# Dilated attention layer: v as two token panels kept on chip, 56 feature tiles in 14 panels, the gates placed behind the keys, three projection banks

## The chip, the cores and the metric

One Trainium2 chip, of which the program uses one core. The time is the device time of one execution in microseconds, the median of several executions. Engines are named as the profile names them: PE (TensorE), PEld (its weight loads), ACT (ScalarE), DVE (VectorE), POOL (GpSimd), SP (SyncE, which here only starts transfers). PSUM, where PE writes, has eight banks of 128 partitions by 512 float32.

## The reference, cut to what matters

Four layers run one after the other on 512 tokens of width 1024: a mixer, a mixture of experts, a short convolution, and the dilated attention layer that the change is about. That last one computes, with h the normalised and modulated input:

```python
def dilated_mixer(h, w_in, w_out, cos, sin):
    B, S, _ = h.shape                       # 1, 512
    G, H, Dh = len(DIL_RATES), DIL_HEADS, DIL_HEAD_DIM      # 3, 8, 128
    E = H * Dh
    q, k, v, z = jnp.split(h @ w_in, [G * E, 2 * G * E, 2 * G * E + E], axis=-1)
    q = apply_rope(q.reshape(B, S, G, H, Dh), cos, sin)
    k = apply_rope(k.reshape(B, S, G, H, Dh), cos, sin)
    v = v.reshape(B, S, H, Dh)
    ...   # per rate g: banded attention of q[g], k[g], v; the three mixed by softmax of their log-denominators
    y = o.reshape(B, S, E).astype(h.dtype) * jax.nn.silu(z)
    return y @ w_out
```

So each head needs eight products of 1024 x 128 weights with the input: three queries, three keys, one v and one gate z. A gated residual and a last normalisation follow.

## The kernel before

Weights come in panels of 2 MB (128 partitions x 4096 float32), number 114 (`P_DIL`) to 129 for this layer's input projection, 130 and 131 (`P_DO`) for its output projection. SP's queue loads them in order into the four slots of `ring`; `load` (L1956) waits until the last chunk of the panel that lay in the slot before has been read. A panel has four chunks. ACT copies each chunk to a rounded high part (`hi`, L746) and DVE computes the rest (`lo`, L1171), into two buffers that alternate, so chunk c can be split only when PE is done with chunk c-2.

PE knows two ways to use a panel. `feature_tiles` (L288) gives the result by feature: a chunk is 128 output columns, and a tile is 24 matmuls (8 of the high part, 8 of the low part, 8 of the high part against the input's low part) of 512 moving columns into one bank. `token_panel` (L306) gives it by token: four tiles of 128 tokens by 512 output columns that fill four banks together, a chunk being 256 rows of the weights; 96 matmuls of 512 columns in all. `lead_panel` (L267) does the first two feature tiles of a layer in step with the arrival of its input.

In the dilated layer each head has two panels, so eight feature tiles in the order q0 q1 q2 z, k0 k1 k2 v. They go alternately to banks 0 and 1; `proj_free` lets a tile start when the tile two before it has been read out of its bank. A query or key tile is read by `rope`: ACT copies the two halves crosswise into `sw` (L1092, L1093), DVE multiplies the bank by the cosine (L1753), `sw` by the sine (L1754) and adds (L1757) into `qkd`. The z tile is read by ACT with Silu. The v tile comes out by feature and is needed by token: ACT copies it to `sw` (semaphore `vc`), PE transposes it in four pieces into bank 5 (L704, semaphore `vt`), and ACT copies it again to `vk` (L1144). PE waits for `vc` straight after the tile's matmuls, and PE works in the order of its program.

Attention of head h-1 is cut into six steps, which stand behind the first six of head h's eight tiles. Step 0 is the score matmuls of query block 0 (three matmuls, which a row shows as six instructions), step 1 is scores of block 1 and `flip` of block 0 (four transposes of the softmaxed scores, L645), steps 2 and 3 are `values` (four matmuls, eight instructions), `flip` and `scores`, step 4 `values` and `flip`, step 5 `values`. Between scores and flip stand `softmax` on DVE (L1765 to L1779) with the exponential on ACT (L1098) in its middle; between flip and values ACT copies the turned scores (L1106). ACT and DVE run the same sequence: for each tile first the split of the next chunk, then `rope`, then the attention step. Each works in the order written. Head 7's six steps follow the last tile, with no tile between them, and the output projection (two token panels) follows those.

Of the kernel before, what the change touches and what calls it, by code (L numbers as in the profile page):

```python
# [15 lines left out]
NE = 32  # L16
# [22 lines left out]
sw ra rb qk z vc vt vk scr att fl pt av  # L39
""".split()  # L40

FEAT = {*range(0, 2), *range(P_C0, P_CO), *range(P_DIL, P_DO)}
# [16 lines left out]
def program(nc, A, out):  # L59
    ctx = ExitStack()  # L60
    with ctx:
# [79 lines left out]
        for i in range(P_C0, N_PANELS):  # L141
            settle(i, free_ring[(i - P_C0) % RING])

# [81 lines left out]
        vk = [area(7168 + 512 * j, 4, 128) for j in range(2)]  # L225
# [19 lines left out]
        TOKENS = [2, 3, 4, 5, 6, 7, P_CO, P_CO + 1, P_DO, P_DO + 1]  # L245
# [8 lines left out]
        def tensor_program(pe):  # L254
# [51 lines left out]
            def token_panel(i, ops, b, nb=None):  # L306

                NH, NL, WH, WL = ops
                for n, ch in enumerate(ORDER.get(i, (0, 1, 2, 3))):
# [3 lines left out]
                    if n == 3:  # L313
# [3 lines left out]
                        for t in range(4):  # L317
                            for kk in range(2):
                                k, o = 2 * ch + kk, ps[:, b + t, :]
# [6 lines left out]
                    for kk in range(2):  # L326
# [3 lines left out]
                        for t in range(4):  # L330
                            mm(ps[:, b + t, :], NH[:, k, t * 128:(t + 1) * 128], h[:, kk, :], n == 0 and kk == 0, False)
                    pe.wait_ge(S["lo"], c + 1)
                    for kk in range(2):
                        for t in range(4):
                            mm(ps[:, b + t, :], NH[:, 2 * ch + kk, t * 128:(t + 1) * 128], lo[:, kk, :], False, False)
                    if nb is not None:
                        pe.wait_ge(S["nl"], nb + 2 * n + 2)
                    for t in range(4):
                        for kk in range(2):
                            x = mm(ps[:, b + t, :], NL[:, 2 * ch + kk, t * 128:(t + 1) * 128], h[:, kk, :], False, False)  # L340
# [307 lines left out]
            def values(h, p):  # L648
                ob = 6 + h % 2
                if p == 0:  # L650
                    pe.wait_ge(S["vk"], h + 1)
# [3 lines left out]
                for q in range(4):  # L655
                    t = mm(ps[:, ob, p * 128:(p + 1) * 128], vk[h % 2][:, q, :], PT[:, q * 128:(q + 1) * 128],
# [15 lines left out]
            def proj_free(g):  # L672

                h, j = g // 8, g % 8
                if j == 3:
                    pe.wait_ge(S["z"], h + 1)
                elif j == 7:
                    pe.wait_ge(S["vc"], h + 1)
                else:
                    pe.wait_ge(S["ra"], 6 * h + (j if j < 3 else j - 1) + 1)  # L680

            for h in range(8):
                i = P_DIL + 2 * h

                def first(j, h=h):
                    if 8 * h + j >= 2:
                        proj_free(8 * h + j - 2)

                def behind(j, h=h):
# [1455 lines left out]
```

## Time and profile before

| | us |
|---|---|
| three runs | 1642.13, 1641.99, 1640.69 (median 1641.99) |
| the profiled execution, whole | 1646.2 |
| its span (first to last instruction) | 1644.4 |
| PE busy, share of the span | 1402.5, 85% |
| DVE busy | 658.6, 40% |
| ACT busy | 484.5, 29% |
| dilated layer, from its third projection tile to its first output-projection matmul | 1133.90 to 1584.20 |
| mean granted TensorE clock over the span | 0.936 of full |

The profiled execution is one more execution, 4.2 us over the median. Times of rows below are microseconds from the start of its span. A row "x8" is eight instructions merged, from the start of the first to the end of the last; matmuls overlap, so the pace of a run of matmuls is read from the starts of neighbouring rows. The granted clock is a share of 2.4 GHz; 0.50 is 1.2 GHz.

### The profile page before, as it was taken

What the parts mean: (1) busy time and instruction counts of PE and PEld (TensorE: products, weight loads), DVE (VectorE), ACT (ScalarE), POOL (GpSimd) and SP (SyncE); (2) the same over time, 40 slices, a digit from 0 to 9 for tenths busy, and PEclk for the clock granted to TensorE, in tenths of its full rate; (3) what the DMA queues carried; (4) which work ended last, traced back from release to release, by engine and by line L of the source; (5) the groups of instructions that cost most, each with busy time, mean ns of one, the idle gap of its engine ahead of it and who ended that gap; (6) DMA issues with size and microseconds to landing.
All of it is one profiled execution on the core that took longest, in us unless ns stands there. A gap on an engine that the chain in (4) does not pass through costs nothing.

```text
span 1644.4 us, 17162 instructions
## 1 busy us (share of the span) xinstructions
PE 1402.5 (85%) x6530; PEld 944.2 (57%) x6530; DVE 658.6 (40%) x1136; ACT 484.5 (29%) x718; POOL 93.6 (6%) x155
## 2 busy tenths in 40 slices
PE   6999985697876778977728999988999999999976
PEld 5786774232222223322216888766788788878765
DVE  4552887000000000000044756455546554655545
ACT  5452512010000000100044231324445444443432
POOL 2000010110000000100020110000000000000000
PEclk9998996899898889998969999999999999999988
DMA  9720279899999999999964553221221212121001
GB/s 354 299 103 1 92 253 382 307 375 401 393 403 386 398 383 401 382 381 396 410 253 186 205 211 133 74 108 51 68 87 64 91 52 102 52 103 52 1 1 64
DMA packets 39852, 347.71 MB, mean 211 GB/s; under 512 B 5952, under 2 KB 6080, under 8 KB 21440
## 3 DMA queue, kind: packets, MB, share of 16 engines
q1 hardware_dynamic: 26176, 292.11, 45.5%
q0 software_dynamic: 12608, 51.42, 9.2%
q10 hardware_dynamic: 960, 2.70, 0.4%
q8 instruction: 73, 1.20, 0.3%
q14 instruction: 35, 0.29, 0.0%
HBM read 321.56 MB, written 24.64 MB: 211 GB/s over the span
## 4 chain that ended last, share of the span: by engine, by line
PE 44%; DVE 3%; ACT 2%; issue 1%; DMA 1%; DVEq 0%; POOL 0%; SPq 0%; ACTq 0%; POOLq 0%
PE ps L256 43%; PE ps L645 1%; ACT ar L794 0%; DVE b_NL L1238 0%; DMA ar<-y_scratch,rt 0%; DVE ar L1230 0%; PE ps L704 0%; DVE hres L1643 0%; ACT ar L807 0%; PE ps L262 0%; DVE hres L1636 0%; DMA y_scratch<-ar 0%; ACT b_NH L803 0%; DVE ar L1823 0%; ACT ar L1008 0%
## 5 line engine op out<-in xcount | busy, mean ns | idle before, releaser
L256 PE MATMUL ps<-ar 128*128 128x128 f32 (+6 forms) x1038 | 251.0, 442 | 30.5 <-ACT ar L938 8.5
L256 PE MATMUL ps<-ring,ar 128*64 128x512 f32 x720 | 220.6, 637 | 55.3 <-issue 48.7
L256 PE MATMUL ps<-b_NH,b_WH 128*128 128x512 f32 x768 | 201.7, 399 | 12.0 <-ACT b_NH L803 6.2
L1585 DVE TENSOR_TENSOR ar<-ar,ps 128x256 f32<-128x256 f32 x34 | 14.3, 421 | 483.1 <-ACT ar L935 483.1
L256 PE MATMUL ps<-b_NH,b_WL 128*128 128x512 f32 x768 | 195.2, 390 | 0.0
L256 PE MATMUL ps<-b_NL,b_WH 128*128 128x512 f32 x768 | 189.7, 389 | 0.0
L256 PEld LDWEIGHTS ps<-ring,ar 128*64 128x64 f32 x720 | 68.8, 147 | 194.0 <-issue 185.9
L1171 DVE TENSOR_TENSOR b_WL<-ring,b_WH 128x1024 fp32r<-128x1024 f32 x112 | 136.7, 1221 | 98.1 <-ACT b_WH L746 98.0
L256 PEld LDWEIGHTS ps<-ar 128*128 128x128 f32 (+3 forms) x1038 | 125.6, 175 | 83.2 <-issue 53.8
L256 PEld LDWEIGHTS ps<-b_NH,b_WH 128*128 128x128 f32 x768 | 141.1, 189 | 42.8 <-ACT b_NH L803 11.1
L256 PEld LDWEIGHTS ps<-b_NH,b_WL 128*128 128x128 f32 x768 | 144.7, 188 | 30.2
L256 PEld LDWEIGHTS ps<-b_NL,b_WH 128*128 128x128 f32 x768 | 144.1, 188 | 30.0
L746 ACT ACTIVATE b_WH<-ring 128x1024 fp32r<-128x1024 f32 x112 | 118.0, 1054 | 136.5 <-PE ps L256 134.2
L256 PE MATMUL ps<-spare,ar 128*64 128x512 f32 x528 | 126.0, 629 | 23.9 <-issue 18.1
L941 ACT ACTIVATE ar<-ps 128x512 f32<-128x512 f32 x34 | 20.3, 597 | 338.9 <-DMA y_scratch<-ar 303.5
L256 PEld LDWEIGHTS ps<-spare,ar 128*64 128x64 f32 x528 | 40.7, 144 | 100.7 <-issue 92.4
L1753 DVE TENSOR_TENSOR ar<-ps,gate 128x512 f32<-128x512 f32 x48 | 33.1, 690 | 94.3 <-ACT ar L1093 93.9
L262 PE MATMUL ps<-ident,ar 128*128 128x128 f32 x128 | 24.2, 363 | 47.8 <-ACT ar L1012 29.3
L807 ACT ACTIVATE ar<-ps 128x512 f32<-128x512 f32 x52 | 30.6, 597 | 107.1 <-PE ps L256 107.0
L1092 ACT ACTIVATE ar<-ps 64x512 f32<-64x512 f32 x48 | 28.5, 594 | 113.7 <-PE ps L256 112.3
L1171 DVE TENSOR_TENSOR a_WL<-ring,a_WH 128x1024 fp32r<-128x1024 f32 x32 | 39.0, 1222 | 54.1 <-ACT a_WH L746 54.1
L256 PE MATMUL ps<-a_WH,a_NH 128*128 128x512 f32 x192 | 56.0, 399 | 4.7 <-DVE a_NL L1394 2.3
(252 smaller groups left out, 1563.1 us busy)
## 6 DMA issues: line engine op xcount, KB each, us to landing
ring<-in_wts_dram SPq DMA_DIRECT2D x80, 2048.0 KB, 15.5
spare<-in_wts_dram SPq DMA_DIRECT2D x30, 2048.0 KB, 36.8
ar<-in_wts_dram SPq DMA_DIRECT2D x22, 2048.0 KB, 37.7
ar<-in_wmod_dram POOLq DMA_DIRECT2D x16, 768.0 KB, 6.0
ar<-in_wmod_dram POOLq DMA_DIRECT2D x24, 512.0 KB, 4.1
y_scratch<-gate POOLq DMA_DIRECT2D x11, 1024.0 KB, 21.2
y_scratch<-ar SPq DMA_DIRECT2D x68, 128.0 KB, 31.2
hres<-in_x_dram SPq DMA_DIRECT2D x4, 512.0 KB, 5.8
```

Source lines behind the costliest of these rows:

```text
L256: return pe.matmul(o, l, m, start=start, stop=stop, skip_group_check=True)
L262: t = pe.transpose(ps[:, banks[k], p * 128:(p + 1) * 128], x[:, p, k * 128:(k + 1) * 128], ident[:, :])
L645: t = pe.transpose(ps[:, 4, q * 128:(q + 1) * 128], Sb[p % 2][:, q * 128:(q + 1) * 128], ident[:, :])
L746: act.activation(chunk_dst(buf, c, feat), chunk_src(i, n), ACT.Copy).then_inc(S["hi"], 1)
L807: act.activation(dst, ps[:, bank, :], func).then_inc(S[sem], 1)
L941: return act.activation(ysb[s], ps[:, b, :], ACT.Copy)
L1092: act.activation(w[0:64, :], o[64:128, :], ACT.Copy)
L1171: dve.tensor_tensor(chunk_dst(ops[3], c, feat), chunk_src(i, n), f32(chunk_dst(ops[2], c, feat)), ALU.subtract).then_inc(S["lo"], 1)
L1585: return dve.tensor_tensor(hh[s], sg[s], ps[:, b, 256:512], ALU.mult)
L1753: dve.tensor_tensor(q, o, cosT, ALU.mult).then_inc(S["ra"], 1)
```

## The change

- The columns of v leave the feature panels. v is computed with two `token_panel`s (`P_V` = 115 and 116), behind the first feature panel. ACT copies their eight results to `vall`, which lies in a ring slot that takes no more panels; the projection's panels take turns in the other three slots. The four transposes of each head, both of its v copies and the semaphores `vc` and `vt` go away. The first scores wait for all eight v copies; the v matmuls of the attention read `vall`.
- The other 56 feature tiles fill 14 panels, seven tiles for each head, q0 q1 q2 k0 k1 k2 z. Heads 6 and 7 have only their six, and the two last tiles are z of head 6 and z of head 7. Attention of head h starts (step 0) behind its own z tile; steps 1 to 5 stand behind q0 to k1 of the next head. Head 6's steps 0 to 5 stand behind head 7's six tiles, head 7's steps 0 and 1 behind the two last z tiles, and its steps 2 to 5 follow the last tile. DVE's last multiplication for head 6 moves behind its softmax of head 7, block 0.
- The tiles go in turn to three banks (0, 1, 5), so a tile waits for the read-out of the one three before it.
- SP loads panel 117 behind the cosine and mask tables, not ahead of them. On POOL a branch of the expert layer gets one more wait, for the transfer before.

Cut to its core (the loops of ACT and DVE that go away are in the listing above):

```diff
-FEAT = {*range(0, 2), *range(P_C0, P_CO), *range(P_DIL, P_DO)}
+P_V = P_DIL + 1
+FEAT = {*range(0, 2), *range(P_C0, P_CO), P_DIL, *range(P_V + 2, P_DO)}
...
-        for i in range(P_C0, N_PANELS):
+        for i in range(P_C0, P_DIL):
             settle(i, free_ring[(i - P_C0) % RING])
+        for i in range(P_DIL, N_PANELS):
+            settle(i, free_ring[(2, 3, 0)[(i - P_DIL) % 3]])
...
-        vk = [area(7168 + 512 * j, 4, 128) for j in range(2)]
+        vall = ring[:, free_ring[1], :].rearrange("p (t e) -> p t e", t=4)
...
+        TILES = [(h, r) for h in range(8) for r in range(7) if h < 6 or r < 6] + [(6, 6), (7, 6)]
+        PROJ = (0, 1, 5)
+
+        def tile_panel(g):
+
+            return P_DIL if g < 4 else P_V + 1 + g // 4
+
+        def step_behind(g):
+
+            h, r = TILES[g]
+            if g == 54:
+                return 7, 0
+            if g == 55:
+                return 7, 1
+            if r == 6:
+                return h, 0
+            if h == 7:
+                return 6, r
+            return h - 1, r + 1
...
                     pe.wait_ge(S["qk"], 6 * h + 6)
+                if a == 0:
+                    pe.wait_ge(S["vk"], 8)
...
-                    pe.wait_ge(S["vk"], h + 1)
...
-                    t = mm(ps[:, ob, p * 128:(p + 1) * 128], vk[h % 2][:, q, :], PT[:, q * 128:(q + 1) * 128],
+                    t = mm(ps[:, ob, p * 128:(p + 1) * 128], vall[:, q, h * 128:(h + 1) * 128], PT[:, q * 128:(q + 1) * 128],
...
             def proj_free(g):
-                h, j = g // 8, g % 8
+                h, r = TILES[g]
+                if r == 6:
+                    pe.wait_ge(S["z"], h + 1)
+                else:
+                    pe.wait_ge(S["ra"], 6 * h + r + 1)
...
+            def first(j):
...
-                    lead_panel(i, op_b, N_DL, (0, 1, 0, 1))
-                    run(feature_tiles(i, op_b, (0, 1, 0, 1), (2, 3), first))
-                else:
-                    for j in feature_tiles(i, op_b, (0, 1, 0, 1), range(4), first):
-                        attention(h - 1, j)
-                for j in feature_tiles(i + 1, op_b, (0, 1, 0, 1), range(4), behind):
-                    if j == 3:
-                        pe.wait_ge(S["vc"], h + 1)
-                        if h:
-                            pe.wait_ge(S["vk"], h)
-                        for q in range(4):
-                            t = pe.transpose(ps[:, 5, q * 128:(q + 1) * 128], sw[(7 * h + 6) % 2][:, q * 128:(q + 1) * 128],
-                                             ident[:, :])
-                        t.then_inc(S["vt"], 1)
-                    if h and j < 2:
-                        attention(h - 1, 4 + j)
-            for step in range(6):
+                    proj_free(0)
+
+            def behind(g):
+                if g >= 7:
+                    proj_free(g - 3)
+
+            b4 = tuple(PROJ[g % 3] for g in range(4))
+            lead_panel(P_DIL, op_b, N_DL, b4)
+            run(feature_tiles(P_DIL, op_b, b4, (2, 3), first))
+            token_panel(P_V, op_b, (2, 3, 4, 6))
+            proj_free(3)
+            pe.wait_ge(S["vk"], 2)
+            token_panel(P_V + 1, op_b, (7, 0, 2, 3))
+            proj_free(1)
+            proj_free(2)
+            for q in range(1, 14):
+                i = P_V + 1 + q
+                b4 = tuple(PROJ[(4 * q + j) % 3] for j in range(4))
+                for j in feature_tiles(i, op_b, b4, range(4), lambda j, q=q: behind(4 * q + j)):
+                    h, step = step_behind(4 * q + j)
+                    if h >= 0 and step < 6:
+                        attention(h, step)
+            for step in range(2, 6):
                 attention(7, step)
-            proj_free(62)
-            proj_free(63)
+            proj_free(54)
+            proj_free(55)
             pe.wait_ge(S["att"], 9 * 31 + 2)
             token_panel(P_DO, op_b, 0, N_DO)
             pe.wait_ge(S["pt"], 32)
-            pe.wait_ge(S["vk"], 8)
             pe.wait_ge(S["y"], 16)
             token_panel(P_DO + 1, op_b, 4)
...
-            def sw_free(h, u):
...
+            def rope(g):
+                h, r = TILES[g]
+                m = 6 * h + r
+                w, o = sw[m % 2], ps[:, PROJ[g % 3], :]
+                act.wait_ge(*tile_done(tile_panel(g), g % 4))
+                if m >= 2:
+                    act.wait_ge(S["qk"], m - 1)
                 act.activation(w[0:64, :], o[64:128, :], ACT.Copy)
                 act.activation(w[64:128, :], o[0:64, :], ACT.Copy).then_inc(S["sw"], 1)
+
+            def silu_z(g):
+                h = TILES[g][0]
+                if h >= 2:
+                    act.wait_ge(S["y"], 8 + h - 1)
+                evict(tile_panel(g), g % 4, zT[h % 2], ACT.Silu, "z", PROJ[g % 3])
...
+            for g in range(4):
+                if g < 2:
+                    hi(P_DIL, g + 2)
+                elif g == 3:
+                    hi(P_V, 0)
+                rope(g)
+            for c in range(2):
+                for n in range(4):
+                    next_hi(P_V + c, n)
+                for t in range(4):
+                    evict(P_V + c, t, vall[:, t, c * 512:(c + 1) * 512], ACT.Copy, "vk",
+                          ((2, 3, 4, 6), (7, 0, 2, 3))[c][t])
+            for g in range(4, 56):
+                next_hi(tile_panel(g), g % 4)
+                if TILES[g][1] < 6:
+                    rope(g)
+                else:
+                    silu_z(g)
+                h, step = step_behind(g)
+                if h >= 0 and step < 6:
+                    attention(h, step)
+            for step in range(2, 6):
                 attention(7, step)
-            act.wait_ge(S["wdone"], done(cno(P_DIL + 15, 3)))
+            act.wait_ge(S["wdone"], done(cno(P_DO - 1, 3)))
...
+            def gated_values(h):
+                dve.wait_ge(S["av"], 4 * h + 4)
+                dve.wait_ge(S["z"], h + 1)
+                dve.tensor_tensor(yTd[:, h, :], ps[:, 6 + h % 2, :], zT[h % 2], ALU.mult).then_inc(S["y"], 1)
+
+            for g in range(4):
+                if g < 2:
+                    lo(P_DIL, g + 2)
+                elif g == 3:
+                    lo(P_V, 0)
+                rope(g)
+            for c in range(2):
+                for n in range(4):
+                    next_lo(P_V + c, n)
+            for g in range(4, 56):
+                next_lo(tile_panel(g), g % 4)
+                if TILES[g][1] < 6:
+                    rope(g)
+                h, step = step_behind(g)
+                if h >= 0 and step < 6 and (h, step) != (6, 5):
+                    attention(h, step)
+                if g == 54:
+                    gated_values(6)
+            for step in range(2, 6):
                 attention(7, step)
...
-            for i in range(P_C0 + 1, P_DIL + 4):
+            for i in range(P_C0 + 1, P_DIL + 3):
...
-            for i in range(P_DIL + 4, N_PANELS):
+            for i in range(P_DIL + 3, N_PANELS):
...
+                    pool.wait_ge(S["o_g"], 16 * (NE + j))
...
+    off = [0, 1024, 2048, 3072, 4096, 5120, 7168]
+    order = [(h, r) for h in range(8) for r in range(7) if h < 6 or r < 6] + [(6, 6), (7, 6)]
+    tiles = [dl[:, :, off[r] + 128 * h:off[r] + 128 * h + 128] for h, r in order]
+    fp = [np.concatenate(tiles[4 * q:4 * q + 4], axis=2).reshape(128, 4096) for q in range(14)]
+    wp += fp[:1] + [dl[:, :, c:c + 512].reshape(128, 4096) for c in (6144, 6656)] + fp[1:]
```

## Rows read from the trace of the kernel before

**Rows 1.** Stretch of one head: us, busy PE, PEld, DVE, ACT, POOL, granted clock, DMA.

```profile
1279.50:1335.20 55.70, 54.95 (x271) 44.97 (x269) 31.39 (x67) 25.57 (x37) 0.00 (x0) 1.00 0.21 76
```

**Rows 2.** Chain of waits in order of time: start, length, what; around one v tile.

```profile
1334.16 0.61 ACT ar L807
```

**Rows 3.** PE's waits, 1150 to 1644: total us, times, longest.

```profile
PE ps L645 <- DVE ar L1779: 7.0, 3, 2.9
PE ps L704 <- ACT ar L807: 6.0, 8, 0.7
```

**Rows 4.** Instructions in order of time (start, length, engine); a token panel of the convolution.

```profile
1055.27 1.98 PE L256 MATMUL ps<-b_WH,b_NL 128*128 128x512 f32 x8
1057.08 1.98 PE L256 MATMUL ps<-b_WH,b_NH 128*128 128x512 f32 x8
```

**Rows 5.** Instructions in order of time; v tile of one head and the next tile.

```profile
1276.35 1.98 PE L256 MATMUL ps<-b_NL,b_WH 128*128 128x512 f32 x8
...
1279.48 2.10 PE L256 MATMUL ps<-b_NH,b_WH 128*128 128x512 f32 x8
```

**Rows 6.** Instructions in order of time; end of head 7 and the tail.

```profile
1555.05 1.97 PE L256 MATMUL ps<-b_NL,b_WH 128*128 128x512 f32 x8
...
1558.27 1.47 PE L256 MATMUL ps<-ar 128*128 128x512 f32 x6
...
1561.23 0.94 ACT L1098 ACTIVATE ar<-ar,sm 128x768 f32<-128x768 f32 x1 [2.17 <-DVE sm L1772]
...
1564.87 0.93 ACT L1098 ACTIVATE ar<-ar,sm 128x768 f32<-128x768 f32 x1 [2.61 <-DVE sm L1772]
...
1566.53 1.64 PE L256 MATMUL ps<-ar 128*128 128x128 f32 x8 [2.31 <-ACT ar L1106]
...
1582.48 2.07 PE L256 MATMUL ps<-ar 128*128 128x128 f32 x8 [0.69 <-ACT ar L1106]
...
1584.20 3.59 PE L256 MATMUL ps<-b_WH,b_NH 128*128 128x512 f32 x8
```

**Rows 7.** Instructions in order of time; ACT at a z tile.

```profile
1307.44 1.28 ACT L807 ACT_TABLE_LOAD   x1 [1.51 <-PE ps L256]
...
1308.73 0.60 ACT L807 ACTIVATE ar<-ps 128x512 f32<-128x512 f32 x1
...
1309.84 1.28 ACT L1098 ACT_TABLE_LOAD   x1
...
1311.49 0.94 ACT L1098 ACTIVATE ar<-ar,sm 128x768 f32<-128x768 f32 x1 [0.37 <-DVE sm L1772]
```

**Rows 8.** Instructions in order of time; start of the dilated layer.

```profile
1128.82 3.80 PE L256 MATMUL ps<-b_NL,b_WH 128*128 128x512 f32 x16
...
1132.01 1.23 DVE L1171 TENSOR_TENSOR b_WL<-ring,b_WH 128x1024 fp32r<-128x1024 f32 x1 [3.86 <-ACT b_WH L746]
...
1133.90 2.11 PE L256 MATMUL ps<-b_NH,b_WH 128*128 128x512 f32 x8 [1.29 <-DVE ar L1753]
```

**Rows 9.** Instructions in order of time; tiles of one head with attention steps 0 to 2.

```profile
1286.29 2.08 PE L256 MATMUL ps<-b_NH,b_WH 128*128 128x512 f32 x8
...
1291.84 1.47 PE L256 MATMUL ps<-ar 128*128 128x512 f32 x6
...
1298.52 0.49 DVE L1779 TENSOR_SCALAR ar<-ar,sm 128x512 f32<-128x512 f32 x1
...
1299.07 1.06 PE L256 MATMUL ps<-ar 128*128 128x128 f32 x8
...
1299.96 0.60 PE L645 MATMUL ps<-ident,ar 128*128 128x128 f32 x4
```

**Rows 10.** Stretches of the tail, columns as in rows 1; the slow-clock ones.

```profile
1567.00:1570.00 3.00, 3.00 (x12) 2.48 (x12) 0.14 (x1) 0.60 (x1) 0.00 (x0) 0.50 0.00 0
...
1581.00:1587.00 6.00, 5.31 (x19) 4.33 (x18) 2.41 (x4) 5.17 (x10) 0.00 (x0) 0.50 0.01 3
```

**Rows 11.** Transfers by line, 1120 to 1560: count, size, median us to landing.

```profile
ring<-in_wts_dram SPq DMA_DIRECT2D x14, 2048.0 KB, 7.7
```

More of the change, by code:

```diff
@@ L308, in token_panel @@
                 NH, NL, WH, WL = ops
+                bank = b if isinstance(b, tuple) else (b, b + 1, b + 2, b + 3)
                 for n, ch in enumerate(ORDER.get(i, (0, 1, 2, 3))):
@@ L318, in token_panel @@
                             for kk in range(2):
-                                k, o = 2 * ch + kk, ps[:, b + t, :]
+                                k, o = 2 * ch + kk, ps[:, bank[t], :]
                                 nh, nl = (a[:, k, t * 128:(t + 1) * 128] for a in (NH, NL))
@@ L330, in token_panel @@
                         for t in range(4):
-                            mm(ps[:, b + t, :], NH[:, k, t * 128:(t + 1) * 128], h[:, kk, :], n == 0 and kk == 0, False)
+                            mm(ps[:, bank[t], :], NH[:, k, t * 128:(t + 1) * 128], h[:, kk, :], n == 0 and kk == 0, False)
                     pe.wait_ge(S["lo"], c + 1)
@@ L1114, in attention @@
                     exp_scores(h, step)
-            for h in range(8):
-                i = P_DIL + 2 * h
-                for j in range(4):
-                    if h == 0:
-                        if j < 2:
-                            hi(i, j + 2)
-                        elif j == 3:
-                            hi(i + 1, 0)
-                    else:
-                        next_hi(i, j)
-                    if j < 3:
-                        rope(h, i, j, j)
-                    else:
-                        if h >= 2:
-                            act.wait_ge(S["y"], 8 + h - 1)
-                        evict(i, 3, zT[h % 2], ACT.Silu, "z", 1)
-                    if h:
-                        attention(h - 1, j)
-                for j in range(4):
-                    next_hi(i + 1, j)
-                    if j < 3:
-                        rope(h, i + 1, j, 3 + j)
-                    else:
-                        sw_free(h, 6)
-                        evict(i + 1, 3, sw[(7 * h + 6) % 2], ACT.Copy, "vc", 1)
-                        act.wait_ge(S["vt"], h + 1)
-                        if h >= 2:
-                            act.wait_ge(S["av"], 4 * (h - 1))
-                        act.activation(vk[h % 2].rearrange("p a b -> p (a b)"), ps[:, 5, :], ACT.Copy).then_inc(S["vk"], 1)
-                    if h and j < 2:
-                        attention(h - 1, 4 + j)
@@ L1147, in scalar_program @@
-            for step in range(6):
+            for g in range(4):
[10 more added lines that the diff above has]
+                          ((2, 3, 4, 6), (7, 0, 2, 3))[c][t])
@@ L1745, in vector_program, with rope @@
             dve.wait_ge(S["rope"], 32)
-            def rope(h, i, j, r):
-                m, w, o = 6 * h + r, sw[(7 * h + r) % 2], ps[:, j % 2, :]
+            def rope(g):
+                h, r = TILES[g]
+                m = 6 * h + r
+                w, o = sw[m % 2], ps[:, PROJ[g % 3], :]
                 q = qkd[h % 2][:, r, :]
@@ L1784, in attention @@
                 if step == 5:
[L1785 to L1809 removed]
+                    gated_values(h)
+            def gated_values(h):
[21 more added lines that the diff above has]
+            for step in range(2, 6):
                 attention(7, step)
```

58 lines of the change are left out of this document (4 added, 54 removed).

## Prediction

> **What bounds the kernel now.** I read first which engine fills the dilated layer. A stretch of one head, between two equal points of its schedule, is 55.70 us long, with PE busy for nearly all of it at full clock, DVE for 31.39 and ACT for 25.57 [rows 1]. So a microsecond is won there only if PE does less or stands less. Next, the chain of waits in order of time: it lies on PE throughout the head except at one place, where it passes through an ACT copy of the v tile [rows 2], with PE's transposes of it behind. The list of who waited for whom over the layer says the same in total: PE waited eight times, once per head, for L807 ahead of L704, and the only other waits of size are three for L1779, in the tail of head 7 [rows 3]. PE never waited on a bank in the steady part. That leaves three places for the change to act on: the v detour of each head, the start of the layer, and the tail.
>
> **Matmuls of v: no change.** Before, 64 feature tiles of 24 matmuls make 1536; after, 56 x 24 = 1344 and two token panels of 96 make 1536. The pace by token is 8 matmuls in 57.08 - 55.27 = 1.81 us [rows 4], 0.2266 each. By feature the instructions have the same shape and, as the tail part shows, the same pace. Cost 0.
>
> **The v detour goes.** The last eight matmuls of a v tile start at 1276.35, and at this pace the next tile could start at 1278.16. It starts at 1279.48 [rows 5]. So wait and transposes take 1.32 us of PE's time, seven times. For head 7 the last eight start at 1555.05, the next work could start at 1556.86 and starts at 1558.27 [rows 6]: 1.41. Sum 7 x 1.32 + 1.41 = **10.65 us**, all of it on the path. In return PE gets only constant waits at the v panels. The new ones are `proj_free(3)` and `vk` >= 2 ahead of the second panel. The first two of a token panel's four results are finished 18 and 12 matmuls before its end (4.1 and 2.7 us earlier), and one copy takes 0.60 (the Silu copy of the same shape [rows 7]); ACT has split the next chunk before that. The second copy ends about 2.7 - 0.3 - 0.6 = 1.8 us before PE asks, if ACT was free. Behind it on PE is the whole second panel, so a late copy costs its lateness, once. I take 0; bounds 0 and two copies, 1.2. The eight copies replace sixteen; ACT is not the bound.
>
> **The start of the layer.** Tile 2 starts at 1133.90, released by DVE's reading of tile 0 (L1753), because both use bank 0 [rows 8]. The 16 matmuls before it start at 1128.82 and end their issue 16 x 0.2266 later, at 1132.45. With a third bank tile 2 needs only its high part, ready before 1132.01, where DVE starts on it released by ACT, and, 1.81 us into the tile, its low part, ready at 1132.01 + 1.23 = 1133.24 against 1134.26 [rows 8]. Gain 1133.90 - 1132.45 = **1.45 us**. Tile 3 then waits for bank 0, which is free at 1133.9, four microseconds early. Bounds: 0 if something else of tile 2 is late, 1.45 at most. Elsewhere the third bank gives nothing, since PE waited for no bank.
>
> **The tail.** Before, PE ends its last tile at 1556.86; without the detour (1.41, counted above) it needs until 1582.48, the values of the last block [rows 6]: 24.21 us with almost nothing beside them. After, steps 0 and 1 lie behind the two z tiles. Scores of block 0 are paid on PE behind tile 54: 1286.29 - 1279.48 - 24 x 0.2266 = 1.37 [rows 5, 9]. Let U be the end of tile 55. Scores of block 1 start at U, DVE reduces them and asks for the exponential at U + 2.96, as from 1558.27 to 1561.23 [rows 6]. But ACT must first do the Silu of tile 55: table load 1.28, copy 0.60, table load 1.28 [rows 7], begun about 0.3 after the tile's end (an ACT copy starts at 1292.04 for a tile that ends its issue at 1286.29 + 24 x 0.2266 = 1291.73 [rows 9]; the next group starts at 1291.84, so the pace holds by feature too). With the small gaps between them that is U + 3.6, later than 2.96 by 0.6. From this exponential to values of block 0 took 1566.53 - 1564.87 = 1.66, and from there to the end of the tail 1582.48 - 1566.53 = 15.95 [rows 6]. New tail: 3.6 + 1.66 + 15.95 = 21.2. Gain 24.21 - 21.2 - 1.37 = **1.6 us**. The multiplication of head 6 (L1787, about 0.7) that moves behind DVE's softmax of head 7 lies beside tile 55.
>
> What I have no row for is the clock in the new tail. Before, it was at 0.50 (1.2 GHz) for two stretches, around 1567 to 1570 and 1581 to 1587, behind sparse work, and at 1.00 between [rows 10]. The second one costs, at values, 1584.20 - 1582.48 = 1.72 [rows 6] against 0.89 at full clock (1299.07 to 1299.96 [rows 9]), and at the next eight matmuls 3.59 [rows 6] against 2.08 [rows 9]: 2.3 us, and about 0.4 at the flip ahead of them. The first costs by the same doubling 0.8 at values, about 0.4 at a flip and 0.2 of the scores before it ends. With both gone the tail is 4.1 shorter. With the middle slow too (a flip and scores, 0.4 + 1.4) and the scores of block 1 (1.4, of which 0.6 lie beside the table load) it is 1.8 + 0.8 = 2.6 longer. I take the same two stretches: 0, bounds -4.1 and +2.6. The new tail has a PE gap of U + 1.8 to U + 5.3, longer than the 2.31 that stood before values of block 0 [rows 6]. The Trainium skill (TensorE: Matmul & The Clock Gate, Part 1) calls the throttled state the default and says that activity releases it; by that rule the longer gap speaks against the change, and the sum would go to its +2.6 end. No row shows a gap at that place.
>
> Table loads: rows show a load of 1.28 with the copy starting 0.01 after it, and the next load 1.28 starting as soon as ACT is free, with the exponential waiting 0.37 for DVE, not for ACT [rows 7]. The Trainium skill (ScalarE: Activation LUTs, What ACT_TABLE_LOAD costs) adds about 1.38 us of drain to each switch. By it the two switches behind tile 55 would put the tail 2.8 us later and the time at 1631.1. The trace disagrees.
>
> **The seven-tile order.** Per head DVE loses one split and keeps the rest, so about 30.2 of 55.70 - 5.44 - 1.32 = 48.9 us. What can break is the time from a tile's end to its flip. Of block 1: the tile ends before the scores at 1291.84, ACT's crosswise copies start at 1292.04, DVE ends the softmax at 1298.52 + 0.49 = 1299.01, and PE asks for the flip at 1299.96 [rows 9]: 0.95 to spare. The order q0, q1, q2 with steps 1 to 3 keeps this pattern; step 3 had the z tile, where DVE had nothing but softmax, and now has a rope. There PE has `values`, `flip` and `scores` (0.9 + 0.4 + 1.4), a tile (5.44) and `values` again ahead of the flip, 9.0 us, and the chain of 1299.01 - 1291.73 = 7.3 fits with more to spare. The gate goes behind the keys, so scores of block 0 come a whole tile (5.44) after k2, whose rope needs about 3.3. Cost 0; bounds 0 and, as the rival below, a wait at each flip.
>
> **Panels.** Three slots in place of four. A panel is asked for when the third one before it is split, lands 7.7 us later (median) [rows 11], and is needed two panels later, over 40 us. Panel 117 moves on SP's queue behind the `hres` wait and the two tables; those waits are over when the layer starts, and 117 then waits for the last chunk of 114 (low part near 1136.4), and is needed behind most of two panels of 21.8 us. Cost 0. POOL's extra wait is on a transfer that had to be read before the wait ahead of it was passed: 0.
>
> **Sum.** 10.65 + 1.45 + 1.6 = 13.7 us, of the profiled execution's 1646.2, which leaves 1632.5. That execution is 4.2 over the median of the three runs; against 1641.99 it gives **1628.3**.
>
> **Rivals.** (a) The tail's clock stays up: 1628.3 - 4.1 = 1624.2. For it: one part of the sparse stretch is shorter; against: the longer gap. (b) The tail gains nothing, by a clock that is low for longer, or by more time at the table switches: 1628.3 + 2.6 = 1630.9. (c) The wait comes back at the v panels, or tile 2 gains nothing: 1.2 to 2.7 more, up to 1631.0. With (b) the lesser of them gives 1632.1. (d) Slower: DVE's chain becomes the bound in the seven-tile order. If each of the 32 flips came later than PE asks, the gain is gone at 13.7/32 = 0.43 us each, which is 0.95 + 0.43 = 1.4 us more chain than now; at 1.6 us more it is 0.65 x 32 = 20.8 us lost, and 1649.1 comes out. For it: fewer tiles to hide the same softmax, no easy z tile at step 3. Against: 62% DVE load and the spare time above. (e) The change does not do what it says, PE waits elsewhere for what it no longer waits for at L704: within 0.2%, about 1641.
>
> **Chances.** Forecast (1626.5 to 1630) 0.55; (a) 0.13; (b) 0.16; (c) 0.09; (d) 0.03; (e) 0.04. A difference of 0.2% (3.3 us) is about what a measurement of this kernel can tell from none. (a), (b), (c) and the forecast are faster: 0.93; same 0.04, slower 0.03. The range takes in (a), (b), (c) and about 0.4 us of scatter: 1624.0 to 1632.5.
>
> **What would show it.** Right: no rows of L704; one head takes about 48.9 us between equal points; PE busy without a gap from tile 2 to tile 55; L1753 releases nothing at the start; the list of PE's waits holds only the tail, with a first gap of about 3.5 us behind flip of block 0. Wrong: PE idle before L645 with L1779 as releaser inside the heads (d); PE idle at the first matmul of the second v panel (c); a slow clock elsewhere than before in the tail (a, b). A chain that no longer lies on PE between the heads would overturn the whole sum.

## The result and the profile after

| | before | after |
|---|---|---|
| median of the runs, us | 1641.78 (8 runs, 1637.08 to 1644.0) | 1628.72 (8 runs, 1624.55 to 1635.83) |
| ratio, with 95% interval | | 0.9933 (0.9911 to 0.9955) |
| profiled execution, its span | 1644.4 | 1622.8 |

The forecast was 1628.3. The kernel is faster by 0.67%, and the interval of the ratio does not reach 1. The two profiled executions differ by 21.6 us of span, though, more than the 13.1 of the medians. So I measure the layer by itself, from one mark ahead of everything that the change does on PE to one behind it. Its stretch L runs from the last 16 matmuls of the lead panel [rows 8, the first row] to the second group of eight of the output projection. Instructions of after in order of time (start, length, engine, what):

```profile
1121.71 3.79 PE L280 MATMUL ps<-b_NL,b_WH 128*128 128x512 f32 x16
1123.72 1.06 ACT L766 ACTIVATE b_WH<-ring 128x1024 fp32r<-128x1024 f32 x1 [3.49 <-PE ps L280]
...
1125.34 1.98 PE L280 MATMUL ps<-b_NH,b_WH 128*128 128x512 f32 x8
```

```profile
1537.46 1.98 PE L280 MATMUL ps<-b_NL,b_WH 128*128 128x512 f32 x8
...
1539.52 1.28 ACT L827 ACT_TABLE_LOAD   x1 [1.59 <-PE ps L280]
...
1540.82 0.60 ACT L827 ACTIVATE ar<-ps 128x512 f32<-128x512 f32 x1
...
1541.43 1.28 ACT L1118 ACT_TABLE_LOAD   x1
...
1542.73 0.93 ACT L1118 ACTIVATE ar<-ar,sm 128x768 f32<-128x768 f32 x1
...
1544.38 1.50 PE L280 MATMUL ps<-ar,ring 128*128 128x128 f32 x8 [3.20 <-ACT ar L1126]
...
1561.59 1.68 PE L280 MATMUL ps<-ar,ring 128*128 128x128 f32 x8 [0.69 <-ACT ar L1126]
1562.93 3.27 PE L280 MATMUL ps<-b_WH,b_NH 128*128 128x512 f32 x8
...
1566.04 1.99 PE L280 MATMUL ps<-b_WL,b_NH 128*128 128x512 f32 x8
```

And the mark that ends L in before, behind 1584.20 [rows 6]:

```profile
1587.63 2.00 PE L256 MATMUL ps<-b_WL,b_NH 128*128 128x512 f32 x8
```

With U the end of the last feature tile's issue (start of its last eight matmuls + 1.81), this gives, in us:

| | L | last 16 to tile 2 | tile 2 to U | U to the mark |
|---|---|---|---|---|
| before | 1587.63 - 1128.82 = 458.81 | 5.08 | 422.96 | 30.77 |
| after | 1566.04 - 1121.71 = 444.33 | 3.63 | 413.93 | 26.77 |

L fell by 14.5, and the rest of the 21.6, 7.1 us, lies ahead of the layer, where PE does the same work in both kernels; the 13 profiled executions below show that this start scatters by more than that. The rest of this text works with L and its three parts.

PE's waits from 1090 on in after (total, times, longest); L704 is gone, and what answers to [rows 3] is all in the tail, the rest belongs to the start of the layer:

```profile
PE ps L286 <- ACT ar L787: 6.0, 2, 5.1
PE ps L672 <- DVE ar L1791: 5.0, 2, 2.9
PE ps L280 <- ACT ar L1126: 3.9, 2, 3.2
PE ps L280 <- DVE b_NL L1248: 2.5, 2, 1.7
PE ps L280 <- ACT b_NH L823: 1.5, 1, 1.5
```

The chain in order of time, one head and the first piece of the next. It no longer leaves PE as it did in [rows 2], and the same point comes back after 1276.61 - 1227.77 = 48.84 us. A head of the kernel before took 55.74 (rows under e1):

```profile
1227.77 25.38 PE ps L280 x116
1253.15 0.44 PE ps L672 x4
1253.58 6.38 PE ps L280 x32
1259.96 0.44 PE ps L672 x4
1260.39 7.67 PE ps L280 x38
1268.06 0.44 PE ps L672 x4
1268.50 7.67 PE ps L280 x38
1276.17 0.44 PE ps L672 x4
1276.61 25.38 PE ps L280 x116
```

The clock in the tail of after, columns as in [rows 1]; three stretches at 0.50, where before had two [rows 10]:

```profile
1545.00:1548.00 3.00, 3.00 (x11) 2.20 (x10) 0.00 (x0) 0.60 (x1) 0.00 (x0) 0.50 0.00 0
1549.00:1551.00 2.00, 0.81 (x8) 0.62 (x6) 1.32 (x6) 0.58 (x1) 0.00 (x0) 1.00 0.00 0
1552.00:1558.00 6.00, 5.25 (x18) 4.05 (x18) 2.01 (x8) 0.68 (x2) 0.00 (x0) 0.50 0.00 0
1559.00:1562.00 3.00, 1.07 (x7) 0.83 (x8) 1.12 (x4) 1.06 (x3) 0.00 (x0) 1.00 0.01 3
1562.00:1566.00 4.00, 4.00 (x15) 3.42 (x15) 2.69 (x5) 4.00 (x9) 0.00 (x0) 0.57 0.00 0
```

### The profile page after: what moved, and what is told of

Read it like the earlier page. It is cut to its first block, busy times and chain, and to the rows that moved or that the text cites. A ratio compares the mean times of both kernels' runs of the same rounds, so it can differ in the third digit from the quotient of the medians.

```text
span 1622.8 us, 17059 instructions
## 1 busy us (share of the span) xinstructions
PE 1406.9 (87%) x6498; PEld 949.3 (58%) x6498; DVE 659.1 (41%) x1136; ACT 481.3 (30%) x710; POOL 95.0 (6%) x155
## 4 chain that ended last, share of the span: by engine, by line
PE 59%; issue 4%; DVE 3%; ACT 3%; DMA 3%; POOL 0%; DVEq 0%; SPq 0%; ACTq 0%; POOLq 0%
PE ps L280 57%; DMA spare<-in_wts_dram 2%; PE ps L672 1%; ACT ar L958 1%; ACT ar L814 1%; DVE b_NL L1248 0%; DVE ar L1595 0%; ACT ar L955 0%; PE ps L533 0%; DVE ar L1240 0%; DMA ar<-y_scratch,rt 0%; DVE hres L1653 0%; ACT b_NH L823 0%; PE ps L286 0%; DVE ar L1836 0%
## 5 line engine op out<-in xcount | busy, mean ns | idle before, releaser
L280 PE MATMUL ps<-ar 128*64 128x512 f32 (+6 forms) x782 | 217.4, 493 | 23.2 <-DVE ar L1563 8.2
L280 PE MATMUL ps<-b_NH,b_WH 128*128 128x512 f32 x704 | 187.1, 401 | 8.3 <-DVE b_NL L1248 4.5
L280 PE MATMUL ps<-b_NH,b_WL 128*128 128x512 f32 x704 | 181.2, 393 | 0.0
L280 PE MATMUL ps<-b_NL,b_WH 128*128 128x512 f32 x704 | 173.6, 389 | 0.0
L280 PEld LDWEIGHTS ps<-b_NH,b_WH 128*128 128x128 f32 x704 | 130.6, 190 | 37.2 <-ACT b_NH L823 9.0
L280 PEld LDWEIGHTS ps<-b_NH,b_WL 128*128 128x128 f32 x704 | 133.8, 190 | 28.0
L280 PEld LDWEIGHTS ps<-b_NL,b_WH 128*128 128x128 f32 x704 | 132.1, 188 | 27.5
L280 PEld LDWEIGHTS ps<-ar 128*64 128x64 f32 (+3 forms) x782 | 92.3, 169 | 72.3 <-issue 50.1
L961 ACT ACTIVATE ar<-ps 128x512 f32<-128x512 f32 x34 | 20.3, 597 | 334.0 <-DMA y_scratch<-ar 296.5
L1106 ACT ACTIVATE ar<-ps 64x512 f32<-64x512 f32 x48 | 28.6, 595 | 99.1 <-PE ps L280 98.5
L280 PE MATMUL ps<-b_WH,b_NH 128*128 128x512 f32 x192 | 55.6, 397 | 1.4 <-ACT b_NH L1084 1.4
```

The lines of the kernel that those rows point to most:

```text
L280: return pe.matmul(o, l, m, start=start, stop=stop, skip_group_check=True)
L961: return act.activation(ysb[s], ps[:, b, :], ACT.Copy)
L1106: act.activation(w[0:64, :], o[64:128, :], ACT.Copy)
```

## The experiments

All of them, with L and its parts as above (us). Each L comes from one profiled execution. Ratios are given where several rounds were run (e1, e8, e10, e11); the other versions ran once, so their verdicts rest on L and the rows. How far L repeats is known for the changed kernel alone, from its two profiles (0.02 us, e11).

| | L | to tile 2 | to U | to the mark |
|---|---|---|---|---|
| before | 458.81 | 5.08 | 422.96 | 30.77 |
| after | 444.33 | 3.63 | 413.93 | 26.77 |
| e1, before without the v detour | 445.25 | 5.08 | 412.78 | 27.39 |
| e2, after with two banks | 445.32 | 5.08 | 414.06 | 26.18 |
| e3, after with gates in place | 445.80 | 3.64 | 412.59 | 29.57 |
| e4, after with the last Silu late | 445.67 | 3.63 | 413.93 | 28.11 |
| e5, after with filler in the tail | 439.34 | 3.63 | 413.93 | 21.78 |
| e6, after, DVE + 0.6 a softmax | 444.67 | 3.62 | 414.29 | 26.76 |
| e7, after, DVE + 1.2 a softmax | 450.58 | 3.63 | 417.66 | 29.29 |
| e8, three gates last | 438.27 | 3.63 | 415.72 | 18.92 |
| e9, before with filler | 455.95 | 5.08 | 422.94 | 27.93 |
| e10, e8 with filler | 435.96 | 3.63 | 415.72 | 16.61 |
| e11, after once more | 444.31 | 3.63 | 413.93 | 26.75 |

**e1: the detour alone**

```diff
                 for j in feature_tiles(i + 1, op_b, (0, 1, 0, 1), range(4), behind):
-                    if j == 3:
-                        pe.wait_ge(S["vc"], h + 1)
...
-                        for q in range(4):
-                            t = pe.transpose(ps[:, 5, q * 128:(q + 1) * 128], sw[(7 * h + 6) % 2][:, q * 128:(q + 1) * 128],
-                                             ident[:, :])
-                        t.then_inc(S["vt"], 1)
...
-                        evict(i + 1, 3, sw[(7 * h + 6) % 2], ACT.Copy, "vc", 1)
...
+                        evict(i + 1, 3, vk[h % 2].rearrange("p a b -> p (a b)"), ACT.Copy, "vk", 1)
```

> The kernel before, with one thing left out: v is not transposed. ACT copies the v tile from its bank straight to vk (by feature, so the attention reads the wrong v); PE's four transposes, the copy to sw and the semaphores vc and vt are gone. I compare the stretch L from the last 16 matmuls of the lead panel to the second group of eight matmuls of the output projection: 458.8 us before, 444.3 after. My theory (PE's wait and transposes are all on the path): L falls by 8 x 1.32 = 10.6, to 448.2, and the whole time by 0.65% (ratio 0.9935). Rival (the wait moves: PE waits for the bank, for vk or for a split instead, and the gain of the change comes from its seven-tile order): L stays within 2 us of 458.8, ratio 0.999 to 1.001. Half of the gain, 453, would say that the copies on ACT matter too.

The ratio is 0.9925 (0.9903 to 0.9948); L is 445.25, a fall of 13.6 where 10.6 was expected. The rival is out. The part from tile 2 to U fell by 10.2. Seven of the eight detours lie in it, and nothing else on PE differs there, so one costs 10.2 / 7 = 1.45, not 1.32. The chain of e1 shows the same:

```profile
1312.02 30.77 PE ps L256 x140
...
1366.31 30.77 PE ps L256 x140
```

One head takes 54.29, against 1446.95 - 1391.21 = 55.74 in before, by these rows of its chain:

```profile
1391.21 13.58 PE ps L256 x60
...
1446.95 13.58 PE ps L256 x60
```

The missing 0.13 is in [rows 5]: the eight matmuls that start after the transposes take 2.10 from start to end, those ahead of the detour 1.98, and the next group starts 1.95 later in place of 1.81. In e1 the matmuls at that place run on without it:

```profile
1274.82 1.98 PE L256 MATMUL ps<-b_NH,b_WH 128*128 128x512 f32 x8
```

I had priced the wait up to the start of the next group and not the slower restart of that group. A group behind score matmuls has 2.08 too, with no wait ahead of it [rows 9], so the slower restart comes with the interruption of the stream and not with idle time alone. The tail of e1 is 3.4 shorter though only 1.4 of detour was in it. The other 2.0 is the clock: e1 has one slow stretch, before has two. So e1's L ends 0.9 from that of the whole change, but partly by this kinder clock.

**e2: two banks**

```diff
-        PROJ = (0, 1, 5)
+        PROJ = (0, 1)
...
-                if g >= 7:
-                    proj_free(g - 3)
+                if g >= 6:
+                    proj_free(g - 2)
```

> The changed kernel with projection banks 0 and 1 only, a tile waiting for the read-out of the one two before it (the second v panel uses bank 5 in place of bank 0). My theory (the third bank works only at tile 2 of the layer): tile 2 starts 1.45 us later against the matmuls before it, heads keep 48.84 us, L = 444.3 + 1.45 = 445.8. Rival (with a rope behind every tile from q0 to k2 the third bank is what keeps PE fed): PE waits for L1765 inside the heads, at least 0.5 us in each of 7 heads, L = 449 or more.

Tile 2 starts 5.08 behind the mark in place of 3.63, exactly the 1.45 forecast, and PE waits for DVE's reading of the bank once:

```profile
PE ps L280 <- DVE ar L1763: 1.3, 1, 1.3
```

From tile 2 to U it loses 0.1. So in the seven-tile order too the third bank gives nothing but the start. L rose by 1.0 only, since the tail was 0.6 shorter, with two slow stretches in place of three, although PE does the same work in the same order there.

**e3: gates in place**

```diff
-        TILES = [(h, r) for h in range(8) for r in range(7) if h < 6 or r < 6] + [(6, 6), (7, 6)]
+        TILES = [(h, r) for h in range(8) for r in range(7)]
...
-            for step in range(2, 6):
+            for step in range(1, 6):
```

> The changed kernel with every gate at its own head, also heads 6 and 7, so that head 7's scores of block 0 stand behind its own z tile and steps 1 to 5 follow with no tile beside them. My theory: steps 0 of head 7 still stands behind a tile, the z tile, but nothing lies beside its softmax: flip of block 0 waits about 3.5 us for it. Against the changed kernel, where tile 55 (5.44 us) lies there, PE's work is the same and this wait is added, less the 1.2 of the scores that are then in the tail: L = 444.3 + 1.3 to 3.5 = 445.6 to 447.8. Rival (the two gates at the end gain nothing, since the Silu and two table loads behind tile 55 delay the exponential as much): L = 444.3 within 0.5.

L = 445.80, 1.5 more than after, inside the forecast span. PE waits for the flip of block 0 again (three waits for DVE where after has two). Taken by parts, 413.93 - 412.59 = 1.3 us of PE work that after has ahead of U (the scores of block 0) now lies behind it, and the stretch behind U is 2.8 longer.

```profile
PE ps L666 <- DVE ar L1785: 7.5, 3, 2.9
```

**e4: the Silu of the last gate late**

```diff
-                else:
+                elif g < 55:
                     silu_z(g)
...
             for step in range(2, 6):
+                if step == 4:
+                    silu_z(55)
                 attention(7, step)
```

> The changed kernel with ACT's Silu of the last gate (tile 55) moved behind the last exponential of head 7, so that no table load stands between tile 55 and the exponential of block 1. My theory: that exponential starts 2.96 us after the end of tile 55 in place of 3.45, and all behind it moves by 0.5 if the clock falls as it did: L = 443.8; the moved Silu with its load fills 1.9 us in which ACT waits. Rival (the slow-clock stretches of the tail follow the gaps of PE and not these 0.5 us): L moves by another amount, between -3 and +2, with slow stretches at other places. Rival (a table switch costs more than its 1.28 us row): the exponential starts over 0.5 us earlier.

A miss in the sum and a hit in the order. The exponential of block 1 starts 2.98 after U in place of 1542.73 - 1539.27 = 3.46, and values of block 0 at 4.63 in place of 5.11, the 0.5 that was asked for. This says nothing on the third point, a hidden cost of table switches: the exponential now waits for DVE, so it could not have moved by more. The ACT rows of after, in the section on the result, show it: there is none. But L rose by 1.3, and more of the tail runs at half clock than in after:

```profile
1548.98 0.93 ACT L1118 ACTIVATE ar<-ar,sm 128x768 f32<-128x768 f32 x1 [4.31 <-DVE sm L1786]
...
1550.63 2.04 PE L280 MATMUL ps<-ar,ring 128*128 128x128 f32 x8 [2.71 <-ACT ar L1126]
...
1569.02 2.08 PE L280 MATMUL ps<-ar,ring 128*128 128x128 f32 x8 [0.69 <-ACT ar L1126]
```

The values of block 0 take 2.04 there and 1.50 in after, the last values 2.08 and 1.68. So half a microsecond won by order stands against 1.3 + 0.5 = 1.8 us, which I put down to the clock; e4 is one execution, and e2 shows that the slow stretches can also differ where the order of the tail is the same. That made the clock of the tail the next thing to test.

**e5: filler in the tail**

```diff
+            def fill(n):
+                for _ in range(n):
+                    mm(ps[:, 5, :], ident[:, :], cosT, True, True)
...
+                if h == 7 and step == 2:
+                    fill(2)
...
+                    if h == 7 and step >= 3:
+                        fill(2)
                     flip(h, step - 1)
```

> The changed kernel with matmuls added that nothing reads: in the tail of head 7 PE multiplies the identity with the cosine table into bank 5, two of 512 columns (about 1.7 us at full clock) ahead of values of block 0 and ahead of the flips of blocks 2 and 3, where it waits 3.2, 2.9 and 2.1 us. My theory (the clock falls because PE stands in the tail): the granted clock stays at 1.00 for most of the tail and at the start of the output projection, and L falls by 2 to 4 us although PE has 5 us more work, to 440.3 to 442.3. Rival (the clock falls in the tail whatever PE does in the gaps, or the filler delays what it stands before): slow stretches stay and L rises by 0 to 3.

L fell by 5.0, more than the 2 to 4 forecast, with 5 us more work on PE. The granted clock is 1.00 in the whole tail and at the projection's start:

```profile
1550.00:1556.00 6.00, 5.39 (x30) 3.73 (x30) 2.50 (x10) 2.08 (x4) 0.00 (x0) 1.00 0.01 3
1556.00:1560.00 4.00, 2.79 (x20) 2.22 (x20) 1.84 (x7) 0.60 (x2) 0.00 (x0) 1.00 0.00 0
1560.00:1564.00 4.00, 2.53 (x10) 0.99 (x8) 1.80 (x9) 1.25 (x3) 0.00 (x0) 1.00 0.01 2
1564.00:1568.00 4.00, 3.57 (x20) 3.10 (x21) 2.37 (x4) 4.00 (x9) 0.00 (x0) 1.00 0.00 0
```

The filler pair takes 1.88 and PE still waits 1.2 to 1.5 behind it, so it delays nothing: values of block 0 start 5.11 after U, as in after. The low clock cost after 26.77 - 21.78 = 5.0 us.

**e6 and e7: how much time the heads have to spare**

```diff
+                dve.tensor_tensor(area(7168, 512), gate[:, 0, 0:512], gate[:, 0, 0:512], ALU.add)
                 dve.wait_ge(S["att"], 9 * a + 2)
```

(e7: 1024 columns.)

> The changed kernel with one more DVE instruction in each softmax, behind its two reductions: an addition of 512 columns (0.69 us) into columns of on-chip memory that nothing reads. My theory (0.95 us to spare at the flips inside the heads): no PE wait inside the heads, they keep 48.84 us; in the tail three softmaxes are bare, so L rises by 3 x 0.6 = 1.8, to 446.2. Rival (DVE is near the bound in the seven-tile order): heads grow by 0.5 us or more each, L = 450 or more.

> The same with an addition of 1024 columns (about 1.25 us, 1.2 of path). My theory: now the chain from a tile's end to its flip is 0.2 to 0.3 longer than PE's time to ask, where a rope precedes; one to three flips of each head wait 0.2 to 0.6 us: heads grow to between 49.0 and 50.3, and the tail by 3.5: L = 449 to 458. Rival (the spare time is over 1.3 us, since DVE can catch up at the z tile): heads stay at 48.84, L = 447.8.

e6: heads 0 to 5 stay at 48.84, as forecast. L rose by 0.3 only and not by 1.8, and the 0.3 is not in the tail but ahead of U, in head 6: from its first flip to its second it takes 7.17 in place of 6.81, because the values of block 0 between them come late. Its steps 0 and 1 both stand behind tiles with a rope, where the other heads have the gate at step 0. That would explain it, but was not tested by itself. In the tail PE's waits for the end of the softmax did grow, from 5.0 to 6.8, but it is as long as in after (26.76), with two slow stretches of the clock in place of three.

e7: heads take 1334.81 - 1285.57 = 49.24, L = 450.6, both in the forecast span. The chain of e7 leaves PE once per head:

```profile
1316.22 0.19 ACT ar L1118
1316.41 0.49 ACT ar L1126
1316.90 0.14 issue
1317.04 1.13 PE ps L280 x8
```

The heads' 0.4 is what is left of 1.2 behind 0.8 to spare. It is not the flip that is first late, as I had put it, but values of block 0: its copy by ACT (L1126) stands behind the exponential of block 1, which waits for DVE. In before the same copy ends about 0.8 ahead of values, 0.1 less than the flip's 0.95. So the room of heads 0 to 5 is between 0.6 and 1.2 us of DVE per softmax and that of head 6 is less than 0.6. The change used up neither.

**e9: before with filler**

```diff
+                if h == 7 and step == 2:
+                    fill(2)
...
+                    if h == 7 and step == 1:
+                        fill(1)
                     if step == 1:
                         scores(h, 1)
+                    if h == 7 and step >= 3:
+                        fill(2)
```

> The kernel before with the same kind of matmuls that nothing reads in head 7's steps (one ahead of scores of block 1, two ahead of values of block 0 and of the flips of blocks 2 and 3), to hold the clock at 1.00, so that the tails of both kernels can be compared at one clock. With the filler the changed kernel's tail, from the end of the last tile to the projection's second group, took 21.8 us. My theory: at one clock the order of the change is worth 24.2 - 21.1 - 1.2 = 1.9 in the tail, and the stretch L from the lead panel to the projection falls from 458.8 to 454.2 (tail 30.8 to 26.2). Rival (most of the tail's gain lay in the clock, not in the order): L = 452.5 or less. Rival (the order gives more than 3, hidden by a lower clock after the change): L = 456 or more.

L = 455.95, between theory and second rival. It does not have one clock throughout: the start of the projection is still slow, 1581.83 - 1578.39 = 3.44 for eight matmuls where e5 takes 1567.28 - 1565.35 = 1.93.

```profile
1577.40 1.33 PE L256 MATMUL ps<-ar 128*128 128x128 f32 x8 [0.69 <-ACT ar L1117]
1578.39 3.60 PE L256 MATMUL ps<-b_WH,b_NH 128*128 128x512 f32 x8
1581.83 1.98 PE L256 MATMUL ps<-b_WL,b_NH 128*128 128x512 f32 x8
```

Less those 1.5, its tail is 26.4 and L 454.4, near the 454.2 of the theory. At one clock the tails are then 26.4 - 1.4 (detour) - 1.3 (scores of block 0, which after has ahead of U; 1.3 by e3, I had written 1.2 ahead of the run) = 23.7 in before against 21.8: the order is worth 1.9. This rests on one correction, not on a run with the clock up from end to end. The 1.1 us in which PE waits ahead of the flip of block 0 got no filler.

**e8 and e10: faster versions**

```diff
-        TILES = [(h, r) for h in range(8) for r in range(7) if h < 6 or r < 6] + [(6, 6), (7, 6)]
+        TILES = [(h, r) for h in range(8) for r in range(7) if h < 5 or r < 6] + [(5, 6), (6, 6), (7, 6)]
...
-            if g == 54:
-                return 7, 0
-            if g == 55:
-                return 7, 1
+            if g >= 53:
+                return 7, g - 53
...
-            if h == 7:
-                return 6, r
+            if h >= 6:
+                return h - 1, r
...
-            for step in range(2, 6):
+            for step in range(3, 6):
+                if step == 4:
+                    silu_z(55)
```

> A version meant to be faster: the gates of heads 5, 6 and 7 are the last three tiles, so that step 2 of head 7 (values of block 0, flip of block 1, scores of block 2) has a tile beside the softmax before it too, and the Silu of the last gate is moved behind the last exponential. My theory: the first PE gap of the tail (3.2 us ahead of values of block 0) goes, and of its slow stretches at least the first one: L falls by 3.2 + 1 = 4 to 6 us, to 438 to 440, ratio to the kernel before about 0.989. Rival (what is covered at the front of the tail is given back, because the bank and gate buffers of head 5 are held until its gate is there): L = 443 to 445, with PE waits ahead of values for L1802.

> A version meant to be the fastest: three gates last and the late Silu of e8, with two filler matmuls ahead of each of the flips of blocks 2 and 3 of head 7, where PE still waits 2.9 us. My theory: no slow clock in the tail or at the start of the output projection, which took 3.5 us there: L falls from 438.3 to 435, ratio to the kernel before 0.986. Rival (with only two gaps to fill the clock falls anyway, or the filler delays the flips): L = 437 to 440, ratio 0.989.

The version of e8 holds the late Silu of e4 too. e8: L = 438.27, 6.1 less than after, ratio to before 0.9897 (0.9865 to 0.9929). The gap ahead of values of block 0 is gone and nothing waits for head 5's buffers; two slow stretches are left. e10: L = 435.96, median 1619.4, ratio 0.9858 (0.9835 to 0.9881), as forecast (435 and 0.986), with the clock at 1.00 in the tail. e5 and e10 compare the two orders at one clock: 439.34 - 435.96 = 3.4. So of e8's 6.1 some 2.7 is clock. The waits of e10 are two for DVE, of 1.2, and the last copy of ACT:

```profile
PE ps L670 <- DVE ar L1798: 2.4, 2, 1.2
PE ps L278 <- ACT ar L1131: 0.7, 1, 0.7
```

**e11: after once more**

> The changed kernel once more, unaltered, beside the kernel before on the same chip, to see how far its whole time scatters and which part of it does. My theory: the dilated layer takes 444 us within 1, whatever the execution (only the slow stretches of the tail move), and the scatter of 4 to 6 us lies ahead of the layer; ratio 0.991 to 0.993. Rival (the layer itself scatters, through its panel transfers): L off by more than 2 us, with PE waits inside the heads.

Ratio 0.993 (0.991 to 0.995). L and each of its parts come out as in the first profile within 0.02 us, the tail with its three slow stretches too. The layer began at 1125.15 against 1121.71. Over all profiled executions of all kernels here it began between 1121.7 and 1130.0. So in the executions that were profiled the scatter lies ahead of the layer; the slowest ones of after, near 1635, have no profile. From 300 to 850 us the DMA engines are busy for 0.98 of the time, in both profiles of after. That makes this stretch a candidate, which no run tested.

## Why the prediction was right, point by point

- **Total.** 13.7 forecast for the layer, 14.5 measured in L, 13.1 between the medians. Forecast 1628.3, measured 1628.72. That these two agree to 0.4 is in part luck: single executions of after lie between 1624.55 and 1635.83, and the median of e11 is 1629.96.
- **Matmuls of v.** Right: 96 matmuls by token and the 24 of a feature tile keep 0.2266 each at full clock; no wait at the v panels (rival c is out), no row of L704.
- **The v detour.** The mechanism was right and the term too small. Forecast 10.65. e1 gives 7 x 1.45 + 1.4 = 11.6, the 0.13 of difference in each of the seven being the restart of the group behind the transposes. (The text ahead of the sum calls L1779 the only other wait of size; the same list also has `PE ps L256 <- ACT ar L1106: 3.0, 2, 2.3`, both waits in the tail, and the tail's term did count them.)
- **The start.** Forecast 1.45, measured 5.08 - 3.63 = 1.45, and e2 takes it back exactly. The upper end of its bounds was the right one, and elsewhere the third bank gives nothing.
- **The tail.** Forecast 1.6. Measured: 30.77 - 1.4 - 26.77 - 1.3 = 1.3 as it ran, 1.9 at one clock. By the forecast's own mark, the last values, it is less: these start at 1561.59 - 1539.27 = 22.3 behind U and not at 21.2, so only 0.6 of the 1.3 lies ahead of them. The other 0.7 is the last values and the start of the output projection, which ran at the low clock for a shorter time. The scores of block 0 cost 1.34 (e3), near the 1.37 taken. The gap ahead of values of block 0 was forecast as U + 1.8 to U + 5.3 and is 3.20 long, ending at U + 5.1. Here the step "I take the same two stretches" was wrong: there are three, the middle one new, and they cost 5.0, where the two of before cost 4.4 (its tail of 30.77 less the 26.4 worked out from e9 for the full clock). It was wrong by 0.6, inside the bounds of -4.1 and +2.6. The Trainium skill's rule (TensorE: Matmul & The Clock Gate, Part 1) that activity releases the throttle pointed the right way, and e5 is the case of it that no row had shown: matmuls in the gaps kept 1.00.
- **Table loads.** The exponential starts at U + 3.46 (forecast 3.6), and the rows of after show load, copy, load and exponential with 0.01 to 0.03 us between them: 1.28 + 0.60 + 1.28. The 1.38 us of drain per switch that the Trainium skill states (ScalarE: Activation LUTs, What ACT_TABLE_LOAD costs) would by estimate have put it near U + 6.2. The trace disagrees, and the 1631.1 that followed from it did not come.
- **The seven-tile order.** Right: no wait inside the heads, 48.84 us each (48.9 forecast). The named weak point was the wrong one by a little: values' copy has 0.8 to spare, the flip 0.95 (e7). Head 6, whose steps the change moved behind six tiles with a rope, has the least room (e6). Rival (d) needed 1.4 more chain per step and there was none.
- **Sum of the measured terms.** 11.6 + 1.45 + 1.9 - 0.6 of clock = 14.35, against 14.5; the rest is 0.2 between tile 2 and U (e3 has 412.59 there, e1 412.78). The too small detour and the too kind clock nearly cancel each other.

## What to carry to other kernels

Price a detour to the point where its engine is back at full pace, not only to the first instruction behind it: here that was 0.13 of 1.45 us, seven times. When an engine is full but for one small round trip per tile, a version that leaves the trip out tells what it costs before a whole schedule is rewritten. At a stage with sparse matmuls ahead of a dense one, look at the granted clock first: work that nothing reads in PE's gaps gave 5.0 us, where the orders that were tried are worth 1.9 (after against before) and 3.4 (e10 against e5) at one clock. And where versions differ by a microsecond or less in such a stage, compare them with the clock held up, not as they run.

## What the runs showed of the hardware that I had not expected

- A low clock in a stretch with little PE work can cost as much as the stretch's order can win: 5.0 us of 26.8 in the tail of after, and an edit of half a microsecond can come out with the wrong sign beside it (e4: 0.5 won, 1.8 lost; e6: 1.8 of waits added to the tail, its length unchanged).
- Two profiles of one kernel had it at the same place: in those of after the tail took 26.77 and 26.75, with three slow stretches of which the first begins at U + 5.7 and U + 5.8. Other kernels with the same order there did not: e2 has two stretches. In e4, 0.5 us shorter in order, the first begins near U + 4. What sets the place was not tested.
- Three fillings of about 1.9 us were enough to keep 1.00 in e5; in e9, whose gaps were filled in the same way but for one of 1.1 us, the clock still fell once, at the start of the projection. What decides between the two is open.
